# A hybrid decoder step: the expert weights' ring is filled two slots per transfer

## What is computed

```
def expert_block(args):
    xb, e = args
    gu = xb @ w_gu[e] + b_gu[e]
    gate, up = gu[:, :D_FF], gu[:, D_FF:]
    gate = jnp.minimum(gate, SWIGLU_LIMIT)
    up = jnp.clip(up, -SWIGLU_LIMIT, SWIGLU_LIMIT)
    hmid = (up + 1.0) * gate * jax.nn.sigmoid(SWIGLU_ALPHA * gate)
    return hmid @ w_down[e] + b_down[e]
```

## Time and profile before

| | |
|---|---|
| median of 3 runs | 1356.24 us (1353.52 to 1356.39) |
| profiled execution, its own time | 1356.5 us |
| its span, first to last instruction | 1354.8 us |
| TensorE matmuls busy | 1310.3 us, 97% |
| VectorE, ScalarE, GpSimd busy | 472.8, 190.8, 51.8 us |
| mean granted TensorE clock | 0.986 of full |
| weight loads of the experts | 256 of gate/up, 128 of down, 1 MB each |
| read from memory | 444 MB, of it 403 MB expert weights |

### The profile page before, as it was taken

How to read it: one execution, slowest core, us unless ns; L and a number is a source line. 1 busy time by engine, 2 the same in 40 slices (tenths; PEclk the granted TensorE clock), 3 DMA queues, 4 the chain that set the end, 5 groups by cost and what they waited for, 6 DMA issues and landing times.

```text
span 1354.8 us, 18813 instructions
## 1 busy us (share of the span) xinstructions
PE 1310.3 (97%) x7023; PEld 562.9 (42%) x7023; DVE 472.8 (35%) x987; ACT 190.8 (14%) x328; POOL 51.8 (4%) x139
## 2 busy tenths in 40 slices
PE   6999999989989999999999999999999999999996
PEld 5777766655433333333333333333333333333331
DVE  2083667263462222332222233322223332222244
ACT  2223421322210000000000000000000000000002
POOL 2002011001000000000000000000000000000000
PEclk9999899999979999999999999999999999999999
DMA  9343116329559999999999999999999999999984
GB/s 291 126 157 130 42 60 191 140 73 310 197 223 418 417 418 418 418 418 417 417 417 418 418 418 418 418 417 417 417 418 418 418 418 418 418 417 417 403 342 187
DMA packets 104098, 450.95 MB, mean 333 GB/s; under 512 B 11713, under 2 KB 21003, under 8 KB 71190
## 3 DMA queue, kind: packets, MB, share of 16 engines
q1 hardware_dynamic: 98948, 446.18, 82.4%
q10 hardware_dynamic: 5114, 4.28, 1.2%
HBM read 444.27 MB, written 6.26 MB: 333 GB/s over the span
## 4 chain that ended last, share of the span: by engine, by line
PE 67%; DMA 2%; DVE 1%; SPq 0%; issue 0%; ACT 0%
PE ps L948 31%; PE ps L969 17%; PE ps L926 7%; PE ps L905 6%; PE ps L919 2%; DMA ring<-in_w_gu 2%; PE ps L934 1%; PE ps L913 1%; PE ps L943 1%; PE ps L962 1%; DVE x_tok L1720 0%; SPq L358 0%; DVE x_tok L1692 0%; DVE proj L1674 0%; DVE proj L1677 0%
## 5 line engine op out<-in xcount | busy, mean ns | idle before, releaser
L948 PE MATMUL ps<-ring,proj 128*64 128x512 f32 x2048 | 466.0, 598 | 0.5 <-DMA ring<-in_w_gu 0.5
L948 PEld LDWEIGHTS ps<-ring,proj 128*64 128x64 f32 x2048 | 141.2, 137 | 257.4 <-issue 246.6
L969 PE MATMUL ps<-ring,proj 128*64 128x512 f32 x1024 | 245.5, 601 | 0.9 <-ACT proj L1207 0.9
L1667 DVE TENSOR_SCALAR proj<-ps 128x512 f32<-128x512 f32 x32 | 22.1, 691 | 414.2 <-PE ps L948 414.2
L1692 DVE TENSOR_TENSOR x_tok<-x_tok,ps 96x512 f32<-96x512 f32 x192 | 122.7, 679 | 96.9 <-PE ps L926 96.9
L969 PEld LDWEIGHTS ps<-ring,proj 128*64 128x64 f32 x1024 | 64.8, 136 | 151.5 <-issue 149.2
L926 PE MATMUL ps<-proj 64*96 64x512 f32 x384 | 105.3, 627 | 0.9 <-ACT proj L1211 0.9
L579 PE MATMUL ps<-feat,ring 128*128 128x288 f32 x384 | 99.4, 411 | 0.0
L547 PE MATMUL ps<-feat,ring 128*128 128x288 f32 x384 | 95.7, 412 | 2.0 <-DVEq L1262 2.0
L905 PE MATMUL ps<-proj 96*64 96x512 f32 x384 | 90.5, 607 | 0.0
L547 PEld LDWEIGHTS ps<-feat,ring 128*128 128x128 f32 x384 | 73.9, 193 | 23.3 <-DVE feat L1261 2.3
(11 more groups left out here) (337 smaller groups left out, 863.9 us busy)
## 6 DMA issues: line engine op xcount, KB each, us to landing
ring<-in_w_gu SPq DMA_DIRECT2D x256, 1024.0 KB, 16.5
ring<-in_w_down SPq DMA_DIRECT2D x128, 1024.0 KB, 15.5
ring<-in_w_in SPq DMA_DIRECT2D x12, 2048.0 KB, 9.1
out<-states SPq DMA_DIRECT2D x1, 2048.0 KB, 8.7
ring<-in_w_oa SPq DMA_DIRECT2D x1, 2048.0 KB, 8.8
ring<-in_w_ob SPq DMA_DIRECT2D x1, 2048.0 KB, 10.1
ring<-in_w_out SPq DMA_DIRECT2D x1, 2048.0 KB, 8.0
out<-states ACTq DMA_DIRECT2D x1, 2048.0 KB, 9.5
```

The lines of the kernel that those rows point to most:

```text
L948: last = mm(bank(j // 2)[64 * (j % 2):64 * (j % 2) + 64, :], xgT[:, k % 4, k // 4, :], ring[:, k, 512 * j:512 * j + 512], start=False, sto ...
L969: last = mm(bank(4)[64 * j:64 * j + 64, :], hidT[:, k % 4, 64 * (k // 4):64 * (k // 4) + 64], ring[:, KT + k // 2, n:n + 512], start=False ...
L1667: ts(hid_g, bank(0), SWIGLU_LIMIT, None, ALU.min).then_inc(sg["gate_clipped"], 1)
```

## The change

Gate/up loads and down loads now take two slots each. `gu_pair(e, k)` loads slots k and k + 1 (256 rows, 2 MB) and raises `w_arrived[k]` alone; `down_load(e, k)` does the same for down slots k and k + 1 (512 rows). SP waits until both slots have been used. TensorE waits only at even gate/up slots and at down slots 0 and 2; the counts back stay as they are, one per slot. The order of the loads is unchanged.

```diff
-            def gu_load(e, k):
-                src = w_gu[0, e, 128 * k:128 * k + 128, :] if isinstance(e, int) else \
-                    w_gu[0][bass.ds(e, 1), 128 * k:128 * k + 128, :].rearrange("a p n -> (a p) n")
-                sp.dma_start(ring[:, k, :], src).then_inc(w_arrived[k], 16)
-
             def down_load(e, k):
-                src = w_down[0, e, 256 * k:256 * k + 256, :] if isinstance(e, int) else \
-                    w_down[0][bass.ds(e, 1), 256 * k:256 * k + 256, :].rearrange("a p n -> (a p) n")
-                sp.dma_start(ring[:, KT + k, :].rearrange("p (j n) -> p j n", j=2),
-                             src.rearrange("(j p) n -> p j n", p=128)).then_inc(w_arrived[KT + k], 16)
+                src = w_down[0][bass.ds(e, 1), 256 * k:256 * k + 512, :].rearrange("a (j p) n -> p (a j) n", p=128)
+                sp.dma_start(ring[:, KT + k:KT + k + 2, :].rearrange("p s (j n) -> p (s j) n", j=2), src) \
+                    .then_inc(w_arrived[KT + k], 16)
+
+            def gu_pair(e, k):
+                src = w_gu[0][bass.ds(e, 1), 128 * k:128 * k + 256, :].rearrange("a (j p) n -> p (a j) n", p=128)
+                sp.dma_start(ring[:, k:k + 2, :], src).then_inc(w_arrived[k], 16)
 
             def gu_loads(b, e):
-                for k in range(KT):
-                    sp.wait_ge(sg["gu_used"], GU0 + 8 * b - 8 + k + 1)
-                    gu_load(e, k)
+                for k in range(0, KT, 2):
+                    sp.wait_ge(sg["gu_used"], GU0 + 8 * b - 8 + k + 2)
+                    gu_pair(e, k)
 
             def down_loads(b, e):
-                for k in range(4):
-                    sp.wait_ge(sg["down_used"], DOWN0 + 4 * b - 4 + k + 1)
+                for k in range(0, 4, 2):
+                    sp.wait_ge(sg["down_used"], DOWN0 + 4 * b - 4 + k + 2)
                     down_load(e, k)
...
                 for k in range(KT):
-                    pe.wait_ge(w_arrived[k], 16 * (b + 1))
+                    if k % 2 == 0:
+                        pe.wait_ge(w_arrived[k], 16 * (b + 1))
...
                 for k in range(KT):
-                    if k % 2 == 0:
+                    if k % 4 == 0:
                         pe.wait_ge(w_arrived[KT + k // 2], 16 * b + 32)
```

More of the change, by code:

```diff
@@ L377, in _ @@
                 sp.sem_inc(w_arrived[KT + k], 16)
-            for k in range(4):
-                gu_load(0, k)
+            for k in (0, 2):
+                gu_pair(0, k)
             sp.wait_ge(sg["gB_done"], NCH)
             sp.wait_ge(sg["prompt_stored"], 32)
-            for k in (6, 7):
-                gu_load(0, k)
+            gu_pair(0, 6)
             sp.wait_ge(sg["conv_stored"], 48)
-            for k in range(4):
+            for k in range(0, 4, 2):
                 down_load(0, k)
             sp.wait_ge(sg["mix_done"], 2 * NI)
-            for k in (4, 5):
-                gu_load(0, k)
+            gu_pair(0, 4)
             gu_loads(1, 1)
```

## The result

The changed kernel takes 1361.02 us (median of 10 runs, 1359.18 to 1363.12) where the kernel before takes 1356.21 (10 runs, 1353.52 to 1359.14): a ratio of 1.0036, 95% interval 1.0028 to 1.0044, or 3.8 to 6.0 us slower. The difference is small but clear of the noise. Its profiled execution took 1359.96 us with a span of 1358.2.

What follows compares the result with a forecast made beforehand. The loop was taken as bound by TensorE, the kernel's end as set by the last gate/up load's landing. Loop terms 0, tail 1.9 + 1.7 = 3.6 us, giving 1359.8 us (+0.26%), range 1356.5 to 1365.

Steps and rivals of the forecast that it cites:

- both clocks: In the loop: TensorE's period is 29.83 us a block, the DMA queue's 30.12, slower by 0.29 us a block.
- Fewer waits and issues: In the loop: TensorE waits on six semaphores a block instead of twelve, SP issues half as many transfers; 0 us.
- Later issue and later landing in the loop: In the loop: pairs are issued and complete later, but backlog and lead cover it, 1.8 us to spare at the closest; 0.
- Term (b), the restart: Tail, from block 30's down loads: one piece more, 2.5 us, less a 0.6 us earlier start; last gate/up load 1.9 us later.
- a bound: Upper bound in the tail: no 2 MB load lands in under 8.0 us; if the last pair trails so too, sum 4.3.
- Term (c): Tail, behind the last gate/up load: 16 matmuls instead of 8, 3.60 against 1.94 us, 1.7 us more.
- slower stream: Second rival, in the loop: the stream is a little slower in pairs; +10.5 us at 1%, from 1361 us; chance 0.14.
- The hidden piece: Third rival, tail restart: larger pieces recover lost moving, (b) gives 1.0, sum 2.7 down to 1.7 us; chance 0.20.
- Cheaper transfers: Fourth rival, tail: a cost per transfer is paid half as often, making the kernel faster, under 1356 us; chance 0.08.

Runs made afterwards that it cites:

- the kernel with 4 MB loads: Changed kernel with gate/up in loads of 4 MB, four slots behind one wait: 1375.44 us against 1356.47 for the kernel before, ratio 1.0136.
- single-slot tail: Changed kernel with 1 MB loads and a wait per slot in the last three groups of loads: 1356.79 us against 1356.76 for the kernel before, ratio 0.9999.
- the tail alone in pairs: Kernel before with 2 MB pair loads and pair waits only in the last three groups of loads: 1360.94 us against 1357.31, ratio 1.0032.
- issuing in pairs alone: Kernel before, but SP waits for both slots of a pair before issuing its two 1 MB loads; TensorE waits per slot: 1358.36 us against 1356.76, ratio 1.0014.
- only block 30's down loads in single slots: Changed kernel with only block 30's four down loads as single slots again: 1358.00 us against 1356.47 for the kernel before, ratio 1.0008.
- the change again: The changed kernel measured once more, on the same chip as the kernel with pairs only in the tail: 1362.60 us against 1357.31 before, ratio 1.0036.
- pairs with two loads ahead: Pairs in the loop, single slots in the tail, two gate/up loads of block 31 before block 30's down loads: 1355.47 us against 1356.47 before, ratio 0.9989.
- waiting in pairs alone: Kernel before with its 1 MB loads, but TensorE waits at every even slot for both slots of the pair: 1357.98 us against 1356.76, ratio 1.0012.
- two loads ahead: Kernel before with the first two gate/up loads of block 31 issued ahead of block 30's down loads: 1355.04 us against 1356.47, ratio 0.9990.
- both in loads of 1 MB: Kernel before with loads issued in pairs and waited for in pairs, but still 1 MB each: 1360.47 us against 1356.76, ratio 1.0029.

## Why the prediction was right

**What bounds the kernel.** Both clocks were read rightly. The period of 29.83 us did not move, the queue kept 418 GB/s, and the kernel with 4 MB loads, once its lead was gone, took on just the queue's 30.12 us.

**Fewer waits and issues, 0.** Shown: with half the waits and half the issues TensorE runs the loop without a gap at the same period.

**Later issue and later landing in the loop, 0.** Shown by the single-slot tail (0.9999), and more finely by the time from the issue of the first gate/up load to the first down matmul of block 29, in the eleven profiles other than that of the 4 MB loads. It has two values, and the loop's loads don't decide which:

| granted clock, 380 to 390 us | time | issued slot by slot in the loop | issued in pairs in the loop |
|---|---|---|---|
| 0.50 to 0.58 | 964.3 to 964.4 us | before; the tail alone in pairs | issuing in pairs alone; only block 30's down loads in single slots; the change again; pairs with two loads ahead |
| 0.69 to 0.77 | 962.4 to 962.6 us | waiting in pairs alone; two loads ahead | the change; both in loads of 1 MB; the tail in single slots |

Pairs or not, the loop takes the same to 0.2 us. The lower clock there goes with 2 us more, in either kind of kernel.

In the profile after, gate/up slots 4 and 5 of block 30:

```profile
L362 SPq DMA_DIRECT2D ring<-in_w_gu x1: 373/373/373, 1249.8 to 1249.8; - x1
...
DMA to landing us min/median/max: 23.2/23.2/23.2
```

They land at 1273.0 and are used at 1275.79: 2.8 us to spare where I had 1.8. Most of the difference is the start: this execution had the full clock earlier, so its first pair was issued 1.2 and not 2.3 us later than before's first slot (390.8 against 389.6). What that left was 0.8 at the pair of slots 4 and 5 of block 1, which landed at 409.3 where slot 5 had landed at 408.5, and 0.5 at that of block 30 (1273.0 against 1272.5).

**Term (b), the restart, 1.9.** The late issue by itself is 1.9 us (issuing in pairs alone). In the changed kernel the last load lands 2.5 us later (40.7 against 38.3). The prediction had one piece more, 2.5 us, less a start 0.6 us earlier. The start was only 0.1 earlier: the first pair landed 6.2 + 7.8 = 14.0 us after the first down matmul of block 29, slot 2 before 1301.1 - 1287.0 = 14.1. So what was too small is the landing of the first 2 MB load, 7.8 us and not 7.3. I had this as a bound, from the 2 MB loads of the earlier trace rows, and did not put it in the sum. Seen from the idle queue, the restart comes 2.9 us later (issued 6.2 and not 3.3 us after that matmul), the time from the use of one down slot to that of the next. The last load is late by less than that, since before's queue, restarted with one slot at a time, was not kept full: its slots 0 to 2 landed 2.8 and 3.1 us apart, where a piece takes 2.5.

**Term (c), 16 matmuls behind the last load, 1.7.** Measured 1.70 us (41.83 - 40.13) by waiting in pairs alone.

**The sum.** Predicted +3.6, in the tail of the profile +4.2, in the medians +4.8 (3.8 to 6.0). The mechanism, its places and the sign were right; the sum was too small by the 0.6 of the 2 MB load's start, and by what differs between executions: in the two later profiles with this tail, 1.7 us for a clock of 0.50 in down of block 31 in one, and 1.9 us for a longer dip of the stream in the other. The 2 us of the early clock come and go in both kernels besides. With these the distance between 4.2 and the medians is plausible, but how often each occurs is not measured. That the profile came out at 1359.96 where 1360.1 was forecast is in part luck: the tail was 0.6 longer than forecast and the part ahead of it 0.8 shorter. The median, 1361.02, is 1.2 above the forecast of 1359.8, beyond the band that the prediction gave it (to 1360.5) and at the edge of the one for a slower stream (from 1361). The time alone would not have told the two apart; the period and the rate do.

**The rivals.** A slower stream is out: 418 GB/s in pairs and in loads of 4 MB alike, with two or four rows a megabyte apart in each partition. The rule of the Trainium skill, "DMA: Bandwidth & Descriptors", section "Latency and other measured facts", that rows a large power of two apart cost bandwidth, does not reach this pattern: the stream kept 418 GB/s with rows 1 MB apart inside a partition. The hidden piece is out as well: loads of 1 MB, issued in pairs, did restart at 418 GB/s, yet the last load came 1.8 us later (1326.30 - 1286.27 = 40.03 against 38.26), not 1.0. Cheaper transfers are out: the rate of the long run is the same at 1, 2 and 4 MB. A lone load of 1 MB does take 4.8 us where its moving takes 2.5, so some 2.3 us (an estimate from the earlier trace rows and the rate) stand beside the moving; in a full queue none of it is seen. The 2.0 us that the prediction takes from the Trainium skill for each transfer stand on that page, "DMA: Bandwidth & Descriptors", in the section "Anatomy of one DMA — SWDGE (gpsimd) path", and the table too is of transfers that GpSimd issued; here SP issues them.

## What to carry to other kernels

Where two resources are both nearly full, compare their periods and the lead of one over the other, not their shares: here 0.29 us a block against a few microseconds of lead told that coarser transfers would be free in 30 blocks and cost in two. Here coarser transfers were paid where the stream restarts and where it ends: about one piece of moving (1.9 to 2.5 us) where the queue had run dry, and one piece of computing (1.7 us) behind the last landing. If large transfers are wanted in such a loop, the last groups can stay small, with no cost that could be told here. A small gain, 1.4 us, came from giving a queue that was about to run dry the loads whose memory was free already. To compare two executions within some tenths, measure both from the same instruction: here the parts ahead of it differed by 2 us with a clock that was high or low in either kernel.

## What the runs showed of the hardware

The granted clock fell to 0.50, the level of 1.2 GHz, in tails where TensorE had short waits. After the wait of 1.78 us for the down pair of block 30 the changed kernel was at half clock for about 3.4 us:

```profile
1300.00:1303.50 3.50, 3.29 (x8) 0.69 (x8) 0.00 (x0) 0.00 (x0) 0.00 (x0) 0.51 1.00 396
```

There it was hidden behind the loads. The same fall around 1334 us, behind waits of 1.33, 1.06 and 0.44 us, was on the chain in two of the profiles (both in 1 MB loads, and the tail alone in pairs) and absent in the changed kernel's two, where the last three waits are the same but for some hundredths (1.31, 1.07 and 0.44; 1.33, 1.06 and 0.44). So nearly the same waits cost 1.7 us in one execution and nothing in another, and what decides it is open. In the kernel before, in issuing in pairs alone, and in those with a single-slot restart, the clock was 1.00 from 1290 to 1346 us.

SP's issue of a load took longer behind a long backlog. The loads of the earlier trace rows were issued in 0.33 to 0.52 us; the last two down loads of the kernel before, which landed 22.5 and 24.1 us after they were issued, took 3.86 and 4.05 us to issue. No matmul waited for them, and why they took so long no run shows.
